# The chunked state of a recurrent mixer: one inverse of 128 tokens, or two of 64 and a solution in two steps

## The reference, cut to what matters

```python
def rwkv7_scan(r, w, k, v, a, bvec):
    def step(state, inp):
        r_t, d_t, k_t, v_t, a_t, b_t = inp
        sa = jnp.einsum('bhvk,bhk->bhv', state, a_t)
        state = (state * d_t[:, :, None, :] + sa[..., None] * b_t[:, :, None, :]
                 + v_t[..., None] * k_t[:, :, None, :])
        return state, jnp.einsum('bhvk,bhk->bhv', state, r_t)
```

## Time and profile before

| | |
|---|---|
| time of three runs | 2652.66 us median (2651.44 to 2654.39) |
| the profiled execution | 2652.95 us, of which its span in the profile is 2651.1 us |
| mean granted clock of PE | 0.94 of full speed |
| busy over the span | PE 2338.6 us, DVE 1311.8, ACT 927.6, POOL 732.1 |
| stage of the state, by the trace | from 2003.65 us (first product of tile 0) to 2212.6 us (first matmul of the next stream) |

### The profile page before, as it was taken

One profiled execution on the slowest core, in us unless ns is written; L12 is line 12 of the kernel. 1 busy time (PEld: TensorE's weight loads), 2 busy tenths in 40 slices (PEclk: granted clock), 3 DMA queues, 4 the chain that ended last, 5 costly groups with the idle time before them and its releaser, 6 DMA issues.

```text
span 2651.1 us, 35320 instructions
## 1 busy us (share of the span) xinstructions
PE 2338.6 (88%) x13455; PEld 1920.8 (72%) x13455; DVE 1311.8 (49%) x2171; ACT 927.6 (35%) x1388; POOL 732.1 (28%) x344
## 2 busy tenths in 40 slices
PE   3888647999999997999979999989967888999998
PEld 3777436888888886767767787767636887778877
DVE  3599973433123324568553213456665554542441
ACT  4211143543123313455444323434452222442341
POOL 2122102223222221310133434433102222344342
PEclk7999868999999998999989999999887998999999
DMA  7656301122112221200023323332100001233332
GB/s 250 223 192 213 108 7 58 48 64 75 52 56 63 69 59 52 72 25 1 18 87 87 97 86 95 104 104 80 52 0 1 1 1 43 85 90 92 95 96 87
DMA packets 337222, 204.70 MB, mean 77 GB/s; under 512 B 5918, under 2 KB 335304, under 8 KB 336968
## 3 DMA queue, kind: packets, MB, share of 16 engines
q1 hardware_dynamic: 331915, 194.02, 24.4%
q10 hardware_dynamic: 5180, 8.94, 1.0%
HBM read 200.74 MB, written 2.20 MB: 77 GB/s over the span
## 4 chain that ended last, share of the span: by engine, by line
PE 38%; issue 31%; DVE 15%; POOL 10%; ACT 3%; DVEq 1%; DMA 1%; ACTq 0%; POOLq 0%
PE ps L575 10%; POOL w_lo L517 10%; PE ps L576 10%; PE ps L577 10%; DVE ps L1234 9%; PE ps L2449 1%; PE ps L2447 1%; PE ps L2439 1%; PE ps L1500 1%; DVE n_t L960 1%; DVE m L2608 1%; PE ps L776 1%; ACT w_hi L547 0%; DVEq L2629 0%; DMA x_rows<-in_ctx 0%
## 5 line engine op out<-in xcount | busy, mean ns | idle before, releaser
L517 POOL TENSOR_TENSOR w_lo<-raw,w_hi 128x1024 fp32r<-128x1024 f32 (+1 forms) x253 | 645.2, 2552 | 1523.0 <-ACT w_hi L547 1504.4
L575 PE MATMUL ps<-x_hi,w_hi 128*128 128x512 f32 (+1 forms) x1864 | 683.1, 366 | 67.8 <-DVE x_lo L1137 49.4
L576 PE MATMUL ps<-x_lo,w_hi 128*128 128x512 f32 (+1 forms) x1864 | 669.0, 359 | 0.0
L577 PE MATMUL ps<-x_hi,w_lo 128*128 128x512 f32 (+1 forms) x1864 | 667.2, 358 | 0.0
L547 ACT ACTIVATE w_hi<-raw 128x1024 fp32r<-128x1024 f32 (+1 forms) x251 | 280.9, 1120 | 836.7 <-PE ps L577 830.8
L575 PEld LDWEIGHTS ps<-x_hi,w_hi 128*128 128x128 f32 x1864 | 356.6, 191 | 141.1 <-issue 68.5
L576 PEld LDWEIGHTS ps<-x_lo,w_hi 128*128 128x128 f32 x1864 | 357.3, 192 | 53.0 <-issue 3.8
L577 PEld LDWEIGHTS ps<-x_hi,w_lo 128*128 128x128 f32 x1864 | 356.7, 191 | 51.8
L1401 DVE SCALAR_TENSOR_TENSOR f_a<-ps,prm,f_a 128x511 f32<-128x511 f32 (+2 forms) x176 | 116.1, 681 | 375.6 <-ACT f_b L1367 364.7
L575 PE MATMUL ps<-g_hi,w_hi 128*128 128x512 f32 (+1 forms) x704 | 259.5, 369 | 14.7 <-DVE g_lo L1410 10.5
L576 PE MATMUL ps<-g_lo,w_hi 128*128 128x512 f32 (+1 forms) x704 | 257.6, 366 | 0.0
(11 more groups left out here) (346 smaller groups left out, 3017.1 us busy)
## 6 DMA issues: line engine op xcount, KB each, us to landing
raw<-in_ffn_w_up SPq DMA_DIRECT2D x88, 512.0 KB, 3.8
ada_tail<-in_ada_w SPq DMA_DIRECT2D x22, 1024.0 KB, 8.2
raw<-in_ffn_w_down SPq DMA_DIRECT2D x32, 704.0 KB, 4.5
raw<-in_w_up SPq DMA_DIRECT2D x44, 512.0 KB, 3.8
ada_s<-in_ada_w SPq DMA_DIRECT2D x20, 1024.0 KB, 9.0
raw<-in_conv_w_pw SPq DMA_DIRECT2D x24, 512.0 KB, 4.1
raw<-in_w_down SPq DMA_DIRECT2D x16, 704.0 KB, 4.6
raw<-in_w_in SPq DMA_DIRECT2D x17, 512.0 KB, 3.9
```

The source lines that it names most:

```text
L517: pool.tensor_tensor(M.w_lo[:, slot, 0:K * P], M.raw[:, slot, 0:K * P], M.w_hi[:, slot, 0:K * P].bitcast(F32), ALU.subtract).then_inc(lo_r ...
L575: pe.matmul(o, wh, hi[:, k, t0:t0 + tn], start=(k == 0), stop=False)
L576: pe.matmul(o, wh, lo[:, k, t0:t0 + tn], start=False, stop=False)
L577: return pe.matmul(o, wl, hi[:, k, t0:t0 + tn], start=False, stop=(k == K - 1))
```

## The change

The mask of the first of the four products now keeps only what lies inside each of the two diagonal blocks of 64 tokens, and puts the block that couples the second half to the first beside them (a third use of the same 128 columns). Levels 0 to 5 remain, level 6 is gone. All matrices of the inverse are 128 x 64, each half of the partitions with its own block: every product of a level is two matmuls, one on rows and columns 0 to 63 of the array, one on 64 to 127, both writing to the same bank at partitions 0 to 63 and 64 to 127. The element-wise work of a level has 64 instead of 128 columns for each head. The first of the four products is made in two parts. The transposes of level 0 become such matmuls too. The solution goes in two steps: `x0` and `u` of the first 64 tokens (`half` 0), then `x0` of the second 64, with the coupling block times the first half's `u` added, then its `u`. The second `x0` stands at level 1 of the next tile, the second `u` at level 2, `state` and `y` at level 3 (before: 1), their DVE work at levels 3, 4 and 5 (before: 1 to 4), the transposes of inputs at and behind level 5. A tensor `M.u` is cleared on POOL ahead of the clearing of `M.m4`.

```diff
+
+
+LEVELS = 6
...
-    mask = np.concatenate([strict, upto, strict, upto], 1)
-    levels = []
-    for e in range(7):
+    sb, tb = s % HD, np.arange(HD)[None]
+    blocks = np.concatenate([(sb < tb).astype(np.float32), np.repeat((s < HD).astype(np.float32), HD, 1)], 1)
+    mask = np.concatenate([blocks, upto, strict, upto], 1)
+    levels = [(sb == tb).astype(np.float32)]
+    for e in range(LEVELS):
         b = 1 << e
...
-        self.lv, self.mt = (behind[0][:, 0:6, SEQ + i * P:SEQ + (i + 1) * P] for i in (0, 1))
-        self.inv_t = [behind[1][:, 0:6, SEQ + i * P:SEQ + (i + 1) * P] for i in (0, 1)]
+        self.lv, self.mt = (behind[0][:, 0:6, SEQ + i * HD:SEQ + (i + 1) * HD] for i in (0, 1))
+        self.inv_t = [behind[1][:, 0:6, SEQ + i * HD:SEQ + (i + 1) * HD] for i in (0, 1)]
...
-        return eng.tensor_tensor(M.lv[:, hs, :], M.m4[:, n % 2, hs, 0:P],
-                                 k_level(e).unsqueeze(1).to_broadcast([P, 3, P]), ALU.mult)
+        return eng.tensor_tensor(M.lv[:, hs, :], M.m4[:, n % 2, hs, 0:HD],
+                                 k_level(e).unsqueeze(1).to_broadcast([P, 3, HD]), ALU.mult)
...
+    HALVES = (slice(0, HD), slice(HD, P))
...
+            t0, t1 = slice(n * P, n * P + HD), slice(n * P + HD, (n + 1) * P)
             for hh in hs:
                 r, c = head_rows(hh), hh // 2
-                for q_, (lhs, rhs) in enumerate(((a_t, kk_t), (a_t, r_t), (k_t, kk_t), (k_t, r_t))):
+                pe.matmul(bank(hh, P)[HALVES[0], :], a_t[c][r, t0], kk_t[c][r, t], start=True, stop=True)
+                pe.matmul(bank(hh, HD)[HALVES[1], :], a_t[c][r, t1], kk_t[c][r, t1], start=True, stop=True)
+                for q_, (lhs, rhs) in ((1, (a_t, r_t)), (2, (k_t, kk_t)), (3, (k_t, r_t))):
                     mm = pe.matmul(bank(hh, P, q_ * P), lhs[c][r, t], rhs[c][r, t], start=True, stop=True)
...
-                mm = pe.transpose(bank(3 * gr, P, i * P), M.lv[:, hh, :], ident)
+                for b in HALVES:
+                    mm = pe.matmul(bank(3 * gr, HD, i * HD)[b, :], M.lv[b, hh, :], ident[b, b], start=True, stop=True)
...
-                mm = pe.matmul(bank(3 * gr, P, i * P), M.lv[:, hh, :], M.inv[:, hh, :], start=True, stop=True)
+                for b in HALVES:
+                    mm = pe.matmul(bank(3 * gr, HD, i * HD)[b, :], M.lv[b, hh, :], M.inv[b, hh, :], start=True, stop=True)
...
-            if e < 6:
+            if e < LEVELS - 1:
                 for i, hh in enumerate(hs):
-                    pe.matmul(bank(3 * gr + 1, P, i * P), inv_t[:, hh, :], M.mt[:, hh, :], start=True, stop=True)
+                    for b in HALVES:
+                        pe.matmul(bank(3 * gr + 1, HD, i * HD)[b, :], inv_t[b, hh, :], M.mt[b, hh, :], start=True,
+                                  stop=True)
             for i, hh in enumerate(hs):
-                mm = pe.matmul(bank(3 * gr + 2, P, i * P), M.mt[:, hh, :], inv_t[:, hh, :], start=True, stop=True)
+                for b in HALVES:
+                    mm = pe.matmul(bank(3 * gr + 2, HD, i * HD)[b, :], M.mt[b, hh, :], inv_t[b, hh, :], start=True,
+                                   stop=True)
             T_S.mark(mm, f"inv{e}{gr}{n}")
 
...
-        def x0(n):
-            S_S.after(pe, f"tok2{n}")
-            if n:
-                V_S.after(pe, f"st{n - 1}")
-            t = slice(n * P, (n + 1) * P)
+        def x0(n, half):
+            b = HALVES[half]
+            if half == 0:
+                S_S.after(pe, f"tok2{n}")
+                if n:
+                    V_S.after(pe, f"st{n - 1}")
+            else:
+                S_S.after(pe, f"ua{n}")
+            t = slice(n * P + half * HD, n * P + half * HD + HD)
             for c in C3:
-                for hh in (2 * c, 2 * c + 1):
-                    mm = pe.matmul(by_parity(hh), M.m4[:, n % 2, hh, 2 * P:3 * P], M.tok[:, 2, hh * HD:(hh + 1) * HD],
-                                   start=True, stop=(n == 0))
-                for hh in (2 * c, 2 * c + 1) if n else ():
+                pair_ = (2 * c, 2 * c + 1)
+                for hh in pair_:
+                    mm = pe.matmul(by_parity(hh)[b, :], M.m4[:, n % 2, hh, 2 * P + half * HD:2 * P + half * HD + HD],
+                                   M.tok[:, 2, hh * HD:(hh + 1) * HD], start=True, stop=(n == 0 and half == 0))
+                for hh in pair_ if n else ():
                     r = head_rows(hh)
-                    mm = pe.matmul(by_parity(hh), kk_t[c][r, t], M.z[r, c, :], start=False, stop=True)
-            T_S.mark(mm, f"x0{n}")
-
-        def u(n):
-            S_S.after(pe, f"x0{n}")
+                    mm = pe.matmul(by_parity(hh)[b, :], kk_t[c][r, t], M.z[r, c, :], start=False, stop=(half == 0))
+                for hh in pair_ if half else ():
+                    mm = pe.matmul(by_parity(hh)[b, :], M.m4[:, n % 2, hh, HD:P],
+                                   M.u[:, hh * HD:(hh + 1) * HD], start=False, stop=True)
+            T_S.mark(mm, f"x0{'ab'[half]}{n}")
+
+        def u(n, half):
+            b = HALVES[half]
+            S_S.after(pe, f"x0{'ab'[half]}{n}")
             for hh in H6:
-                mm = pe.matmul(bank(6, HD, hh * HD), M.inv_t[n % 2][:, hh, :], M.x0[:, hh * HD:(hh + 1) * HD],
+                mm = pe.matmul(bank(6, HD, hh * HD)[b, :], M.inv_t[n % 2][b, hh, :], M.x0[b, hh * HD:(hh + 1) * HD],
                                start=True, stop=True)
-            T_S.mark(mm, f"u{n}")
+            T_S.mark(mm, f"u{'ab'[half]}{n}")
...
             for gr, hs in GROUPS:
                 mats(n, gr, hs)
             if n:
-                x0(n - 1)
+                x0(n - 1, 0)
             for gr, hs in GROUPS:
                 first_level(n, gr, hs)
             if n:
-                u(n - 1)
-            for e in range(1, 7):
+                u(n - 1, 0)
+            for e in range(1, LEVELS):
                 for gr, hs in GROUPS:
                     level_times_inv(n, e, gr, hs)
                 if n and e == 1:
+                    x0(n - 1, 1)
+                if n and e == 2:
+                    u(n - 1, 1)
+                if n and e == 3:
                     state(n - 1)
                     y(n - 1)
-                if e == 3:
+                if e == 5:
                     if n:
                         turned(n - 1)
                     tokens(n, 0)
-                if e == 5:
-                    tokens(n, 1)
-                    tokens(n, 2)
                 for gr, hs in GROUPS:
                     inv_step(n, e, gr, hs)
-        V_S.after(pe, "inv613")
-        x0(3)
-        u(3)
+            tokens(n, 1)
+            tokens(n, 2)
+        V_S.after(pe, "inv513")
+        for half in (0, 1):
+            x0(3, half)
+            u(3, half)
         y(3)
...
         for n in N4:
             if n:
-                x0(n - 1)
-                u(n - 1)
-            for e in range(1, 7):
+                x0(n - 1, 0)
+                u(n - 1, 0)
+            for e in range(1, LEVELS):
                 for gr in (0, 1):
                     T_S.after(act, f"mt{e}{gr}{n}")
-                    S_S.mark(act.activation(M.mt[:, 3 * gr:3 * gr + 3, :], heads(bank(3 * gr)), ACT.Copy),
+                    S_S.mark(act.activation(M.mt[:, 3 * gr:3 * gr + 3, :], heads(bank(3 * gr, 3 * HD)), ACT.Copy),
                              f"mt{e}{gr}{n}")
+                if n and e == 1:
+                    x0(n - 1, 1)
                 if n and e == 2:
+                    u(n - 1, 1)
+                if n and e == 4:
                     deviation(n - 1)
-                if n and e == 3:
+                if n and e == 5:
                     turned(n - 1)
-                if n and e == 4:
-                    high_part(n - 1)
-                for q_ in {3: (0,), 5: (1, 2)}.get(e, ()):
-                    tokens(n, q_)
-        for step in (x0, u, deviation, turned, high_part):
+            for q_ in (0, 1, 2):
+                tokens(n, q_)
+            if n:
+                high_part(n - 1)
+        for half in (0, 1):
+            x0(3, half)
+            u(3, half)
+        for step in (deviation, turned, high_part):
...
-        of_last = {1: state_and_variance, 2: normed, 3: gated, 4: low_part}
+        of_last = {3: state_and_variance, 4: normed, 5: gated}
         dve.wait_ge(zero_ready, done(4))
         for n in N4:
             for gr in (0, 1):
                 masked(n, gr)
             for gr in (0, 1):
                 inv_start(n, gr)
-            for e in range(1, 7):
+            if n >= 2:
+                low_part(n - 2)
+            for e in range(1, LEVELS):
                 for gr in (0, 1):
                     inv_sums(n, e, gr)
                 if n and e in of_last:
                     of_last[e](n - 1)
+        low_part(2)
...
+                pool.memset(M.u[:, :], 0.0)
                 pool.memset(M.m4[:, :, :, :], 0.0).then_inc(zero_ready, 1)
```

(54 more changed lines are left out.)

21 lines of the change are left out of this document (11 added, 10 removed).

## The result

The changed kernel takes 2635.53 us (median of five, 2629.11 to 2639.13) beside 2652.86 us for the kernel before: a ratio of 0.9927 (0.9911 to 0.9944). A second set of five, taken later (experiment 7), gave 2631.09 us and 0.9913 (0.9898 to 0.9927). It is faster, by 17 to 23 us, where 44.5 were forecast; the time lies in the range of 2592 to 2640, above the 2596 to 2621 that I gave for the likeliest case.

A forecast was written before the change was run, and what follows sets the result against it. PE was taken to bound a level, with DVE's latency added. Three tiles -34, tile 0 -13.8 and the tail +3.3 gave -44.5 us from 2652.95: 2608 us, range 2596 to 2621.

The forecast's parts named there:

- the likeliest case: Whole kernel: the halves' passes overlap and a level shortens, giving 2608 us, own range 2596 to 2621; chance 0.60.
- the start of a tile: Tile start to level 1's second product: 11.2 us becomes 10.2, DVE and POOL saving 1.8, `mats` adding 0.8.
- much above 5 us: Warning sign: a `mats` of six heads taking much above 5 us would put the time above 2620.
- A set of 0.32 us: Levels: three heads' products as six overlapping pairs of passes at 0.054 us each, 0.32 us a set instead of 0.67.
- A level of 2.7: Levels of the inverse: one level takes 2.7 us instead of 4.82.
- The rest of tile 2: Tile 2 after its start: levels 12.6 us, PE work between products 10.6, DVE's variance work and `normed` 3.1.
- Element-wise work: In a level, at half width: DVE sum 0.55 to 0.35 us, ACT copy 0.49 to 0.33, POOL product 1.02 to 0.53.
- Tail: Solution left over after the last tile: two of each step instead of one, +3.3 us, to 27 us.
- The halves don't overlap: Rival, levels: halves writing one bank run in turn, set 0.64 us, level loop 4.27, total 2631 us; chance 0.22.
- Full price: Rival: each half pass costs a whole one, set 1.33 us, level 7.7, total 2696 us; chance 0.04.
- The clock falls: Rival: half-width matmuls leave PE too idle in a level, holding it at 1.2 GHz; 2653 us, no change; chance 0.07.
- the three woven tiles one gain: Tiles 1 to 3, each with an earlier tile woven in: 36.5 us against 47.8, -11.3 each, three times -34.

The follow-up runs named there:

- experiment 7: The changed kernel run once more, unedited: 2631.09 us, ratio 0.9913 to the kernel before.
- experiment 1: Against the changed kernel, `mats` reordered: in each group of three heads all split 64-column products first, then the nine 128-wide ones; 2607.37 us, ratio 0.9817 to the kernel before.

## Why the prediction was off

**The step that failed** is the one in the start of a tile: "`mats` gains two passes a head and changes of tile shape ... 0.08 a change; three heads ahead of the first mask: +0.8". What failed is the count of what a change does. I priced a wait at each and kept the 0.56 us a head of rows 6, which rested on the next head's passes running beside the last one's on the other rows. Two changes in each head end that. Six wide passes and two pairs of split ones, 0.111 us each alone, are 0.89 us, so 0.33 of the 1.22 us is lost overlap; the other 0.33 is the two changes, 0.17 each and not 0.08. I had charged a change to the products with the state alone, though those behind them pay too, as the chain of before shows:

```profile
2108.89 0.59 PE ps L2504 x4
2109.47 0.45 PE ps L2507 x4
```

Four passes of 128 rows take 0.59 us behind a change and 0.45 without one; with 0.37 for 0.21 that is 0.30 for two changes, 0.15 each. All six heads, not three, then hold up the masks, and the clock fell to 0.50 in the middle. The start of tile 2 came to 16.4 us instead of 10.2, and that of tile 0 to 17.95 (2002.75 to 2020.70 in the second profile, from the first split product to level 1's second set), against 12.61 in experiment 1. That is the shortfall: grouping gives back 24 to 28 us, and the forecast was off by 23 to 27.5. The prediction's last paragraph had named the sign, a `mats` "much above 5 us", as what would put the time above 2620; it took 10.4 in tile 2 (2078.23 to 2088.60).

A rule would have told it. Tiles at 64 x 64 and at 64 x 128 are two shapes, and the Trainium skill (TensorEngine Tiling (Array Packing), Tiling Modes, Key Properties) says that a change of the mode drains TensorE. The trace agrees: 1.22 us a head with two changes, 1.55 us for three heads' wide products with none between, and in experiment 1 the weight loads stand still for 0.17 us where split gives way to wide:

```profile
2065.37 0.29 PEld L2442 LDWEIGHTS ps<-pj,av 64*128 64x128 f32 x2 [0.17 <-issue]
```

Rows 6 and 7 each show overlap within one shape; across a change no row of before did, and I let it stand.

**A set of 0.32 us**: measured 0.35. **A level of 2.7**: 2.84. **The rest of tile 2**, from level 1's start on, 26.3 forecast: 27.9 in the changed kernel (44.3 - 16.4), 27.7 in experiment 1; the second `x0` takes 2.75 us instead of 2.4. **Element-wise work**: DVE's sum 0.36 us (0.35), ACT's copy 0.33, POOL's product 0.60 (0.53). **Tail**: 27.7 us (27).

**The halves don't overlap** is refuted: a set would be 0.64 us. The rule against it, in the Trainium skill (TensorEngine Tiling (Array Packing), Restrictions and Gotchas, Gotcha 1), that tiles on different rows can't use one bank at once, doesn't hold for these tiles, which write different partitions of the bank: 12 passes in 0.35 us, 0.029 each. Passes of the same size that all lie on one half, those of the second `u`, take twice that, 0.059 each at the same clock of 1.00:

```profile
2101.31 0.53 PE ps L2510 x9
```

**Full price** is refuted by the same rows. **The clock falls** was half right, for the wrong place and reason: not in the levels, where a set takes 0.35 us, but in `mats`, and stayed low through the masks, the first `x0` and the start of level 1.

That experiment 1 meets the forecast of 2608 to within 1 us is in part luck. From the first product of a tile to that of the next, in us:

| | tile 0 | tile 1 | tile 2 | tile 3 and tail |
|---|---|---|---|---|
| before | 42.4 | 47.7 | 47.8 | 71.8 |
| forecast | 28.6 | 36.4 | 36.5 | 63.8 |
| changed | 33.5 | 38.8 | 44.3 | 73.5 |
| 1 `mats` grouped | 28.2 | 33.2 | 36.8 | 66.2 |

In experiment 1 tile 1 is 3.2 us shorter than forecast, and the last tile with the tail 2.4 longer; the prediction gave the three woven tiles one gain. (Tile 0 of the kernel before starts at 2002.86, not at 2003.65.)

## What to carry to other kernels

Before a product is split to save columns of the array, look at who runs beside it: a change of tile shape costs 0.17 us here, and no trace shows overlap across one. If the split is needed, issue all products of one shape together, as far as accumulation groups in a bank allow. And two small products in a dense loop can take back much of what they were meant to save (24 to 28 of some 46 us here), so cost the work ahead of the loop with its overlap taken away, too.
